# Storing the transposed activations of a two-block network with the two token tiles interleaved element by element

## The reference

```python
def s5_mixer(h, w_in, ..., w_glu, b_glu, w_out):
    proj = h @ w_in
    ...
    y = y * jax.nn.sigmoid(y @ w_glu.astype(jnp.float32) + b_glu.astype(jnp.float32))
    y = y.astype(h.dtype) * jax.nn.silu(z)
    return y @ w_out

def moba_mixer(h, w_in, q_gain, k_gain, w_out):
    proj = h @ w_in
    q, k, v, z = jnp.split(proj, 4, axis=-1)
    ...
    return (out * jax.nn.silu(z)) @ w_out
```

## Time and profile before

| | |
|---|---|
| time of three runs | 1239.05 us median, 1238.3 to 1243.12 |
| profiled execution, first to last instruction (its span; its whole time is not listed apart) | 1235.8 us |
| median less span | 3.25 us |
| mean granted TensorE clock | 0.995 |
| PE busy | 1205.2 us, 98% |
| PEld busy | 1013.5 us, 82% |
| DVE, ACT, POOL busy | 901.5, 639.1, 100.4 us |
| DMA | 215.68 MB, 175 GB/s |

### The profile page before, as it was taken

The page is one execution under the profiler, slowest core; times in us unless marked ns, Lnnn a source line. Parts: engine busy times, 40 slices in busy tenths (PEclk is TensorE's granted clock), DMA queues, the critical chain, the costliest instruction groups (busy, mean ns, idle before and its releaser), DMA issues.

```text
span 1235.8 us, 19035 instructions
## 1 busy us (share of the span) xinstructions
PE 1205.2 (98%) x7597; PEld 1013.5 (82%) x7597; DVE 901.5 (73%) x1463; ACT 639.1 (52%) x1034; POOL 100.4 (8%) x163
## 2 busy tenths in 40 slices
PE   7999999999999999999999999999999999999998
PEld 3566778888988788787999987988788787999986
DVE  7998877757589998687666655589997687665553
ACT  4334565665556665545444544556575545444441
POOL 6300011101000200201000001000200201000000
PEclk9999999999999999999999999999999999999999
DMA  7635666434565555354766664565445355565552
GB/s 251 221 94 173 205 208 191 156 119 146 163 205 168 155 157 187 133 169 164 216 201 188 193 195 154 174 211 169 158 153 188 132 170 170 190 197 193 191 194 75
DMA packets 71958, 215.68 MB, mean 175 GB/s; under 512 B 16256, under 2 KB 19744, under 8 KB 71744
## 3 DMA queue, kind: packets, MB, share of 16 engines
q1 hardware_dynamic: 65008, 206.37, 52.0%
q0 software_dynamic: 2112, 6.97, 1.8%
q10 hardware_dynamic: 4752, 1.14, 0.4%
HBM read 208.95 MB, written 3.15 MB: 172 GB/s over the span
## 4 chain that ended last, share of the span: by engine, by line
PE 86%; DVE 8%; ACT 3%; issue 2%; POOL 1%; DMA 0%; DVEq 0%; POOLq 0%; ACTq 0%
PE acc L700 17%; PE acc L702 17%; PE acc L701 17%; PE acc L678 7%; PE acc L680 7%; PE acc L679 7%; PE acc L639 3%; PE mixed L1015 1%; DVE weights_lo L1776 1%; PE mixed L1112 1%; ACT junk L1279 1%; PE turned L755 1%; DVE h_T L1806 1%; PE mixed L999 1%; PE mixed L1008 1%
## 5 line engine op out<-in xcount | busy, mean ns | idle before, releaser
L1776 DVE TENSOR_TENSOR weights_lo<-weights_raw,weights_hi 128x1024 fp32r<-128x1024 f32 (+1 forms) x304 | 355.7, 1204 | 71.6 <-ACT weights_hi L1244 71.0
L1244 ACT ACTIVATE weights_hi<-weights_raw 128x1024 fp32r<-128x1024 f32 (+1 forms) x304 | 305.8, 1043 | 80.8 <-DMA weights_raw<-stream_dram 80.6
L700 PE MATMUL acc<-weights_hi,act_F_hi 128*128 128x512 f32 (+1 forms) x680 | 275.7, 406 | 5.6 <-DVE act_F_lo L1806 3.4
L702 PE MATMUL acc<-weights_hi,act_F_lo 128*128 128x512 f32 (+1 forms) x680 | 267.2, 393 | 0.0
L701 PE MATMUL acc<-weights_lo,act_F_hi 128*128 128x512 f32 (+1 forms) x680 | 265.4, 390 | 0.0
L678 PE MATMUL acc<-act_F_hi,weights_hi 128*128 128x256 f32 x624 | 173.6, 278 | 0.0
L679 PE MATMUL acc<-act_F_hi,weights_lo 128*128 128x256 f32 x624 | 172.5, 276 | 0.0
L680 PE MATMUL acc<-act_F_lo,weights_hi 128*128 128x256 f32 x624 | 172.4, 276 | 0.0
L700 PEld LDWEIGHTS acc<-weights_hi,act_F_hi 128*128 128x128 f32 x680 | 128.7, 189 | 34.2 <-DVE act_F_lo L1806 4.3
L702 PEld LDWEIGHTS acc<-weights_hi,act_F_lo 128*128 128x128 f32 x680 | 128.4, 189 | 28.4
L701 PEld LDWEIGHTS acc<-weights_lo,act_F_hi 128*128 128x128 f32 x680 | 128.7, 189 | 25.6
(11 more groups left out here) (339 smaller groups left out, 1923.6 us busy)
## 6 DMA issues: line engine op xcount, KB each, us to landing
weights_raw<-stream_dram SPq DMA_DIRECT2D x306, 512.0 KB, 3.7
weights_raw_more<-stream_dram SPq DMA_DIRECT2D x58, 512.0 KB, 4.3
gains<-rows_dram POOLq DMA_DIRECT2D x12, 512.0 KB, 4.8
weights_raw<-stream_dram SPq DMA_DIRECT2D x6, 416.0 KB, 3.1
weights_raw<-stream_dram SPq DMA_DIRECT2D x4, 384.0 KB, 3.5
x_T<-x_in_dram SPq DMA_DIRECT2D x4, 256.0 KB, 6.0
ssm_bc<-ssm_bc_dram SPq DMA_DIRECT2D x1, 1024.0 KB, 8.6
u_scratch<-u_T ACTq DMA_DIRECT2D x4, 256.0 KB, 5.5
```

What stands on the lines that cost most here:

```text
L700: pe.matmul(o, xh, wh, start=first and kk == 0, stop=False)
L702: i = pe.matmul(o, xl, wh, start=False, stop=last and kk == s["nk"] - 1)
L1244: act.activation(high(s, slice(0, n)), whole(s, slice(0, n)), ACT.Copy).then_inc(hi_made, 1)
L1776: dve.tensor_tensor(low(s, slice(0, n)), whole(s, slice(0, n)), high(s, slice(0, n)).bitcast(F32), ALU.subtract).then_inc(lo_made, 1)
```

## The change

The rows' tensors keep their size and place. Inside each k tile of 256 elements the two token tiles are now in turn: token b of tile 0 at element 2b, token b of tile 1 at 2b + 1. So a stationary tile of rows is every second element (a step of 8 bytes), and spans 1020 bytes of each partition where it spanned 512. In `hidden_slot` the rows are the moving tile and are still read element after element, so its result has its tokens in turn too.

No instruction is added, removed or moved on any engine; operands' access patterns change, and nothing else:

- PE: `tile_slot`'s three loads have step 2. Transposes still read whole tiles, and write PSUM with tile 0's blocks first, then tile 1's.
- ACT and DVE: writes of the high and low rows (L1269, L1296, L1478, L1699, L1800, L1806, L1809) have step 2, in two passes where both tiles are written at once; DVE reads the high half with the same step. The same holds for the attention's output (L1653 and DVE's product with `silu_z_F`) and for the convolution's affine result (L1732).
- ACT reads PSUM with step 2 where a `hidden_slot` result goes back to plain token order, that is in the convolution's two `glu.` chunks (L1336, L1338). The feed-forward keeps its tokens in turn until the next `tile_slot`.

```diff
+        def by_turns(x):
+            return x.rearrange("p k (b t) -> p t (k b)", t=TT)
+        def flat_by_turns(x):
+            return x.rearrange("p (k b t) -> p k t b", b=P, t=TT)
+        def two_tiles(x):
+            return x.rearrange("p (t n) -> p t n", t=TT)
...
@@ tile_slot
-                    xh, xl = (f[:, k, t * P:(t + 1) * P] for f in (hi, lo))
+                    xh, xl = (f[:, k, t::TT] for f in (hi, lo))
...
@@ turn, on PE
-                            i = pe.transpose(turned_bank[n % 2][:, kk * SEQ + t * P:kk * SEQ + (t + 1) * P], src(t, k + kk), ident)
+                            i = pe.transpose(turned_bank[n % 2][:, (nk * t + kk) * P:(nk * t + kk + 1) * P], src(t, k + kk), ident)
...
@@ turn_hi, on ACT
-                    act.activation(dst[:, k0 + k:k0 + k + nk, :], turned_bank[n % 2][:, 0:nk * SEQ].rearrange("p (k t) -> p k t", t=SEQ),
+                    act.activation(by_turns(dst[:, k0 + k:k0 + k + nk, :]), two_tiles(turned_bank[n % 2][:, 0:nk * SEQ]),
...
@@ tile_hi, on ACT
-                act.activation(f_hi[:, 4 * half:4 * half + 4, t * P:(t + 1) * P],
-                               turned_bank[n % 2][:, :].rearrange("p (k t) -> p k t", t=P),
+                act.activation(by_turns(f_hi[:, 4 * half:4 * half + 4, :])[:, t], turned_bank[n % 2][:, :],
...
@@ evac of the convolution's glu, on ACT
-                        act.activation(conv_part(t), b.rearrange("p (k t) -> p k t", t=SEQ), ACT.Copy, scale=0.5).then_inc(read, 1)
+                        act.activation(conv_part(t).rearrange("p k (t b) -> p k t b", t=TT), flat_by_turns(b), ACT.Copy, scale=0.5).then_inc(read, 1)
...
@@ tile_lo, on DVE
-                part = (slice(None), slice(4 * half, 4 * half + 4), slice(t * P, (t + 1) * P))
-                stt(f_lo[part], turned_bank[n % 2][:, :].rearrange("p (k t) -> p k t", t=P), scale,
-                    f_hi[part].bitcast(F32), ALU.mult, ALU.subtract).then_inc(turned_lo, 1)
+                lo, hi = (by_turns(f[:, 4 * half:4 * half + 4, :])[:, t] for f in (f_lo, f_hi))
+                stt(lo, turned_bank[n % 2][:, :], scale, hi.bitcast(F32), ALU.mult, ALU.subtract).then_inc(turned_lo, 1)
...
```

More of the change, by code:

```diff
@@ L793, in turn @@
                         pe.wait_ge(who, value)
-                        for kk in range(min(2, ktiles - k)):
-                            i = pe.transpose(turned_bank[n % 2][:, kk * SEQ + t * P:kk * SEQ + (t + 1) * P], src(t, k + kk), ident)
+                        nk = min(2, ktiles - k)
+                        for kk in range(nk):
+                            i = pe.transpose(turned_bank[n % 2][:, (nk * t + kk) * P:(nk * t + kk + 1) * P], src(t, k + kk), ident)
                     i.then_inc(turned, 1)
@@ L1335, in evac @@
                     elif kind == "glu." and i == 0:
-                        act.activation(conv_part(t), b.rearrange("p (k t) -> p k t", t=SEQ), ACT.Copy, scale=0.5).then_inc(read, 1)
+                        act.activation(conv_part(t).rearrange("p k (t b) -> p k t b", t=TT), flat_by_turns(b), ACT.Copy, scale=0.5).then_inc(read, 1)
                     elif kind == "glu.":
-                        act.activation(conv_t[:, t, :], b, ACT.Tanh, scale=0.5).then_inc(read, 1)
+                        act.activation(conv_t[:, t, :].rearrange("p (k t b) -> p k t b", t=TT, b=P), flat_by_turns(b), ACT.Tanh, scale=0.5).then_inc(read, 1)
                     elif kind == "uq.":
@@ L1477, in y_hi @@
                 b = mixed_of(f"y{part}")
-                act.activation(f_hi[:, 2 * part:2 * part + 2, :], b.rearrange("p (k t) -> p k t", t=SEQ), ACT.Copy,
+                act.activation(by_turns(f_hi[:, 2 * part:2 * part + 2, :]), two_tiles(b[:, :]), ACT.Copy,
                                scale=0.5).then_inc(y_hi_made, 1)
@@ L1652, in attn_out @@
                     b = take(f"attn.o{h}")
-                    act.activation(gF[:, h, :], b[:, 0:SEQ], ACT.Copy).then_inc(outs_copied, 1)
+                    act.activation(by_turns(gF[:, h:h + 1, :]), two_tiles(b[:, 0:SEQ]), ACT.Copy).then_inc(outs_copied, 1)
                     if h == HEADS - 3:
@@ L1752, in _ @@
                     if c == 1:
-                        act.activation(h2_hi[:, 0:2, :].rearrange("p k t -> p (k t)"), take(f"L{l}.f0")[:, :],
+                        act.activation(by_turns(h2_hi[:, 0:2, :]), two_tiles(take(f"L{l}.f0")[:, :]),
                                        ACT.Copy, scale=0.5).then_inc(hid_hi, 1)
@@ L1799, in turn_lo @@
                     nk = min(2, ktiles - k)
-                    dve.scalar_tensor_tensor(out=lo[:, k0 + k:k0 + k + nk, :].rearrange("p k t -> p (k t)"),
-                                             in0=turned_bank[n % 2][:, 0:nk * SEQ], scalar=scale,
-                                             in1=hi[:, k0 + k:k0 + k + nk, :].rearrange("p k t -> p (k t)").bitcast(F32),
+                    dve.scalar_tensor_tensor(out=by_turns(lo[:, k0 + k:k0 + k + nk, :]),
+                                             in0=two_tiles(turned_bank[n % 2][:, 0:nk * SEQ]), scalar=scale,
+                                             in1=by_turns(hi[:, k0 + k:k0 + k + nk, :].bitcast(F32)),
                                              op0=ALU.mult, op1=ALU.subtract).then_inc(turned_lo, 1)
@@ L2525, in mla_out @@
                         dve.wait_ge(turned_hi, highs(n))
-                        tt(mo_lo[:, h // 2, :], turned_bank[n % 2][:, 0:SEQ], mo_hi[:, h // 2, :].bitcast(F32),
+                        pair = slice(h // 2, h // 2 + 1)
+                        tt(by_turns(mo_lo[:, pair, :]), two_tiles(turned_bank[n % 2][:, 0:SEQ]), by_turns(mo_hi[:, pair, :].bitcast(F32)),
                            ALU.subtract).then_inc(turned_lo, 1)
@@ L2598, in _ @@
                         dve.wait_ge(hid_hi, HT // 2 * l + c)
[L2599 to L2602, removed]
+                        lo, hi = h2_lo[:, 2 * c - 2:2 * c, :], h2_hi[:, 2 * c - 2:2 * c, :].bitcast(F32)
+                        if c > 1:
+                            lo, hi = (x.rearrange("p k t -> p (k t)") for x in (lo, hi))
+                            hid = ffn_h[:, (c - 1) % 2, :]
+                        else:
+                            lo, hi = by_turns(lo), by_turns(hi)
+                            hid = two_tiles(mixed_bank[mix_at[f"L{l}.f0"][0] % 2][:, :])
+                        stt(lo, hid, 0.5, hi, ALU.mult, ALU.subtract).then_inc(hid_lo, 1)
                 run(11)
```

16 lines of the change are left out of this document (8 added, 8 removed).

## The result

The changed kernel takes 1247.76 us (median of 5, 1247.0 to 1252.0), the kernel before, beside it on the same chip, 1239.05 us (1235.68 to 1243.12). The ratio is 1.0085, interval 1.0061 to 1.0108: under 1%, but clear of no change. The profiled execution of after has a span of 1246.0 us (before 1235.8), at a granted clock of 0.997 (0.995): the 2.4 GHz level in both, so the clock explains nothing.

The account below looks back on a forecast made before the run. PE, busy 98% of the span, was taken to bound the kernel by its 512-column matmul pitch. All terms were taken as 0: 1235.8 us span + 3.25 around it + 0 = 1239 us, range 1207 to 1265.

Parts of the forecast that it names:

- rival C: Slower: the stepped load, touching 1020 bytes, disturbs the moving read more; 1253 us at 4.6 ns, 1285 at doubled excess; chance 0.16.
- What bounds the kernel: PE's own rate sets the end: 2952 matmuls of 512 columns at 0.229 us, 2.95 us per nanosecond on each.
- The moving side: PE's moving operand: weights untouched, or rows still read element after element over the same 1024 bytes; cost nothing.
- The stationary load, its length: PE's loads with step 2 may take longer but hide behind their matmuls; taken as 0, upper bound 20 us.
- The stationary load beside the moving read: PE's load and moving stream reading SBUF together: taken as 0, bounds a 38 us gain and a 46 us loss.
- Writes of ACT and DVE: Stepped writes and reads on ACT and DVE, mostly off PE's path; taken as 0, up to 14 us.
- The lone matmul: A PE matmul without a load beside it shows 0.40 us, others 0.39: weak evidence against the load slowing it.
- Rival A: Faster: stepped load and moving read advance equally and rarely meet; 1199 us whole, 1225 us in part; chance 0.28.
- Rival B: Slower: the stepped load outgrows its matmul, which then waits; 20 us at the ACT rate, 1259 us; chance 0.14.

Follow-up runs that it names:

- e1: The kernel before with step 2 only in the stationary loads of slot-by-slot products, no write changed; 1245.01 us, ratio 1.0069.
- m1: Kernel without the network: groups of 32 matmuls, sweeping columns, stationary columns, stationary start and step; 512 columns in sequence took 226.7 to 234.2 ns each.
- m3: Kernel without the network: groups of 24 matmuls, varying widths, distances, steps and predecessors; 512 columns at distance 192 took 233.3 or 228.9 ns each.
- e2: The changed kernel with 2304 of the 2952 512-column loads back in sequence, stepped writes kept; 1242.46 us, ratio 1.0032 to the kernel before.
- m2: Kernel without the network: groups of 24 matmuls at 4 moving by 16 stationary starts, step 1 and 2; with the step none below 229.9 ns.

## Why the prediction was wrong

Forecast 1239 us, measured 1247.76; the time lies within the range, and the case that came in is rival C, which had been given 0.16, with its own price of 1253 us at 4.6 ns. By its own sign, a pitch more than 2 ns off, the forecast is wrong. The steps in order:

- *What bounds the kernel* was right: PE's own rate, 2952 matmuls of 512 columns, 2.95 us for each nanosecond. The loss is that pitch: 11.3 us of it, against 1.4 us of everything else that grew.
- *The moving side*, taken as 0: right as far as can be told; the 256-column pitch is 113.5 in both windows. Over the run it is 0.4 ns more (0.9 us), because 330 of the 2483 took the second value and not 122; e1, which leaves these products alone, had 1171 there.
- *The stationary load, its length*, taken as 0: right. 6 ns more (188 to 194) against the 120 of the upper bound; the narrower forms, which leave it less room, moved by less than 3 ns (384 columns 174.9 to 177.2, 416 columns 189.6 in both). The bound was the price of a step of 16 bytes: m1 finds 122 ns more there, and m3 a load that sets the pitch at 233 to 239 ns, where the bound had said 233.5. The page "SBUF — State Buffer" of the Trainium skill (section "Specifications (TRN2)") calls two hits on a line full speed. For DVE that holds to 3 ns; for the load it fails by 6 ns and for ACT's write by 40, small in the sum but not nothing.
- *The stationary load beside the moving read*, taken as 0: this step failed. It measured +4.1 ns on 2727 matmuls and -2.6 on mla_F's 112, 11 us gross. The reason given was that the excess is proportional to the columns, 0.443 and 0.447 ns. m3 shows that this was a coincidence: the two forms stood at different distances, 192 and 64, and at one distance the excess is flat, or grows but not in proportion. From two points, which differed in more than their width, I had read a law, and put it above the one row that compared equal shapes at two addresses: mla_F's 233.6 against 229. That row was the effect of the distance, without a step. That its 4.6 ns is so near the 4.1 of the step is luck: one is the way from distance 192 to 64 in sequence, the other the step at 192, and at 64 the step takes 3 ns off.
- The Trainium skill's "TensorE: Matmul & The Clock Gate", section "Step-by-step: what each phase is for", has two independent SBUF read ports, so that a load takes nothing from the running matmul. The measurement differs: 226.7 to 234.5 ns for one shape, by the distance between the two starts alone. So the two reads are not independent in what the matmul's rate shows. The lone matmul was no evidence; the view's matmul ends are modelled.
- *Writes of ACT and DVE*, taken as 0: right within what e2 can tell. ACT's on act_F_hi are 40 ns longer, and ACT as a whole is busy for 1.8 us more; the waits for the low half are 4.1 us as before.
- *Rival A* rested on both sides advancing 8 bytes for each element. m2 has that equal pace at eight distances and m1 at sixteen: it is never below 229.9 ns. It is false as a mechanism. *Rival B* is excluded at this step (6 ns more, not over 100) and shown at a step of 4; at 8 load and pitch are longer still. *C* was right in kind, in that the step and the address of the load change the pace of the moving read beside it; but its loads' mean did not stay, it rose by 6 ns, and "touches 1020 bytes" isn't what decides, since distance 64 with the step is 230 and without it 233.3.

The 3.25 us between span and median that the forecast adds lay between two executions, not around the span, which has 1.8 us around it; against the later medians of the kernel before, 1236 to 1237 us, the change costs 11 us and not 8.7.

What stays open is the mechanism in the chip: what the two reads share, why it repeats every 256 bytes, and why one distance can have two values. The runs give the table, not its reason.

## What to carry to other kernels

Before reading a law from two rows, make sure that they differ in that one thing only; a row of equal shapes at two addresses weighs more than a proportion between different shapes. When PE is 98% busy, a change of layout is priced by the pitch of its commonest matmul, at the exact addresses it will have: sweep the start of the stationary side over 256 bytes in a kernel of one matmul, with more than one predecessor, before changing the network. A layout's offset serves every form that touches the tensor, so what one gains another may lose.

## What the runs showed that was not expected

- Stretches of float32r matmuls with a 128-column load beside each, in which all intervals are equal to 1 ns, stand at 226.7 and 233.3 ns with 512 columns and at 113.3 and 120.0 with 256: 13.3, 20.0, 6.7 and 13.3 over one column per tick, all multiples of 6.7 ns. The other pitches are means of patterns that repeat over a few matmuls.
- An offset of 128 bytes in an unchanged kernel costs 0.9%, and 64 bytes 0.85%, by way of two different forms.
- A steady run at one distance can have either of two pitches, 117.8 or 113.3 ns for 256 columns at 64, 233.3 or 228.9 for 512 at 192, and the likely reason is what ran before it. In the network the 256-column products mix both: 122, 330 or 1171 of 2483 in the slower one in three executions.
- A stationary load of one element per 16 bytes takes 310 ns against 188 (step of 4), one per 8 bytes 194, though that spans twice the bytes too.
